# A two-layer streaming encoder: the stick-breaking products as three of 64 columns, summed in one bank, and the gate applied in VectorE's last step

## The chip, the cores and the metric

The kernel runs on one core of a Trainium2 chip. The metric is the device time of one execution in microseconds; before the change it is 1565.58 us, the median of 3 runs (1564.21 to 1566.16). What is read below comes from one profiled execution of the same kernel.

## The reference, cut to what matters

The trunk has two layers. The even layer (layer 0) has 4 heads of differential attention and 8 heads of stick-breaking attention, the odd one latent attention. The change touches the stick-breaking heads alone:

```python
z = einsum('bqhd,bkhd->bhqk', qb, ks) * (B_DH ** -0.5)          # B_DH = 64, 8 heads
earlier = pos[None, :] < tq[:, None]
log_skip = where(earlier, log_sigmoid(-z), 0.0)
log_pass = lax.cumsum(log_skip, axis=3, reverse=True) - log_skip
a = where(earlier, exp(log_sigmoid(z) + log_pass), 0.0)
ys = einsum('bhqk,bkhd->bqhd', a, vs).reshape(bsz, L, B_W) * silu(gs)
```

1024 tokens and 16 learned meta tokens make 1040 queries and keys. Everything is float32.

## The kernel before, in words

**Precision.** TensorE multiplies numbers of reduced precision at full rate. So every float32 operand is split into a high part (a rounded copy) and a low part (the rest), and a product is made as high x high, high x low and low x high, added up in a PSUM bank. ScalarE writes the high parts, VectorE the low ones (`ring`, `kst`, `qst`, `vtok`); GpSimd splits the weights of the projections (`wraw` to `wsp`, lines 872 and 873).

**Units and groups.** Layer 0 is worked in 8 units; units 0 to 3 (kind A) are the differential heads, units 4 to 7 (kind B) hold two stick-breaking heads each. A unit has one group for the 16 meta queries and four for pairs of query blocks (0 and 1, 2 and 3, 4 and 5, 6 and 7), and in kind B each of these once per head: 40 groups, numbers 20 to 59. Layer 1 (kind C) has 8 units.

**A kind B group.** TensorE makes the scores (line 1625). ScalarE takes the sigmoid (`tb`, line 1108). VectorE runs a product scan backwards over the keys (`pb`, line 1396); its result is the weight of "not yet taken", and with values replaced by differences of neighbours (GpSimd, `step_values`) the sum over keys gives the output but for the last value (`vlast`). The weights are turned by TensorE in turns of one or two key tiles (line 1649); ScalarE writes the turned high part into `ring` (line 1139), VectorE the low part (line 1411). Then TensorE multiplies (`product`, line 1679) into bank 7 (`PO`). In a kind B group the stationary operand is 128 columns wide: 64 of the values' high part, 64 of their low part. It is multiplied by the high part and by the low part of the weights, two instructions per key tile. Rows 0 to 63 of the bank then hold high values x all weights, rows 64 to 127 low values x all weights. The first turn of a group is the 16-row tile of the meta keys; the others have 128 rows. The last pair of a group has a tile of 256 query columns and one of 128, the other pairs have two of 256.

**The end of a group.** ScalarE copies rows 64 to 127 to `otmp` (`output`, line 1149, behind the semaphore `pv_done`), VectorE adds rows 0 to 63, `vlast` and `otmp` in one instruction per block and writes `ot` (line 1438, semaphore `o_evac`); the next group's first product waits for `o_evac`. After the second head of a pair, GpSimd multiplies 128 rows of `ot` by `gate` (`gate_group`, line 946, semaphore `y_gated`), and SyncE stores them. `gate` is the SiLU of the unit's own projection `g0`, made in three column chunks during the same unit: ScalarE takes the sigmoid (line 1065), VectorE multiplies (line 1283).

**Order.** Each engine runs its own list, in order. The lists come from a planner (`Lines`, `weave`): every step has an estimated duration, the steps that it waits for, and a tail, and the planner advances the engine that can begin first; `RANK` gives the precedence of kinds of step on an engine (S scores, T turning, X product, Y end of a group, G gating, W weight split, P projection's evacuation, p projection). Projection matmuls (line 1553) are put in one by one where TensorE has room. After the last projection of layer 0, GpSimd splits the eight tiles of the output weights (into `big`) and the first tiles of y, which are loaded back from `y_scratch`; then TensorE starts the output projection (line 1703).

## Time and profile before

| what | us |
|---|---|
| median of 3 runs | 1565.58 |
| profiled execution, its own time | 1564.86 |
| its span, first to last instruction | 1563.1 |
| TensorE matmuls busy in it | 1420.8 (91%) |
| VectorE, ScalarE, GpSimd busy | 850.1, 557.2, 525.2 |
| granted TensorE clock, share of full speed | 0.953 |

"Busy" is time in which at least one instruction of the engine runs; matmuls overlap, so the mean duration of one (some 300 ns) is not the distance to the next. That distance is read from a timeline: the start of one row of equal matmuls to the start of the next row, over their count. PE is TensorE, PEld its weight loads, DVE VectorE, ACT ScalarE, POOL GpSimd, SP SyncE. Layer 0's attention ends with the last projection near 711 us and the output projection's start near 750 us; layer 1 follows.

### The profile page before, as it was taken

The numbers are of one execution on the slowest core, as the hardware profiler recorded it, in microseconds if no ns is written. First come the engines' busy times: TensorE is split into PE (matmuls) and PEld (weight loads), VectorE is DVE, ScalarE is ACT, GpSimd is POOL, SyncE is SP. The second block draws the span as 40 slices with busy tenths as digits, with TensorE's granted clock in tenths as the row PEclk, the third lists the DMA queues.
The fourth block names the chain that finished last, engine by engine and source line by source line (L and its number), as shares of the span: only waits on it lengthen the run. The fifth ranks groups of instructions, "written<-read, shape, count | busy, mean of one in ns | idle before, by whom it ended". The sixth has DMA issues, their size and how long they took to land.

```text
span 1563.1 us, 22642 instructions
## 1 busy us (share of the span) xinstructions
PE 1420.8 (91%) x8604; PEld 1289.7 (83%) x8604; DVE 850.1 (54%) x1941; ACT 557.2 (36%) x1267; POOL 525.2 (34%) x426
## 2 busy tenths in 40 slices
PE   6999898989899999997899998998998989898896
PEld 6898797979788988986688997897887979887685
DVE  4666758585576746566244213424666656656243
ACT  3444344443544535253011004333344444434111
POOL 3213121212223042227544332532223222235553
PEclk9999998999999999997899999998999989989898
DMA  5000100000110010103433211111101111112541
GB/s 189 28 28 28 41 28 29 27 28 28 41 35 21 21 48 18 38 18 88 142 132 109 95 55 54 56 62 52 44 29 34 45 38 35 42 41 83 167 148 68
DMA packets 50796, 90.39 MB, mean 58 GB/s; under 512 B 4720, under 2 KB 33648, under 8 KB 50560
## 3 DMA queue, kind: packets, MB, share of 16 engines
q1 hardware_dynamic: 48384, 80.55, 16.0%
q10 hardware_dynamic: 2304, 8.39, 1.3%
q8 instruction: 69, 1.13, 0.3%
q14 instruction: 39, 0.32, 0.1%
HBM read 67.82 MB, written 21.10 MB: 57 GB/s over the span
## 4 chain that ended last, share of the span: by engine, by line
PE 44%; POOL 4%; DVE 4%; ACT 2%; issue 2%; DMA 1%; POOLq 0%; SPq 0%; ACTq 0%; DVEq 0%
PE bank L1553 17%; PE bank L1703 12%; PE bank L1625 7%; PE bank L1679 5%; PE bank L1649 2%; POOL big L873 2%; POOL big L872 1%; ACT rtmp L1079 1%; DVE qpe L1313 1%; PE bank L1576 1%; DVE qpe L1309 1%; DVE rtmp L1259 1%; DMA wraw<-y_scratch 1%; DVE rtmp L1257 0%; DVE rtmp L1258 0%
## 5 line engine op out<-in xcount | busy, mean ns | idle before, releaser
L1553 PE MATMUL bank<-big,wsp 128*128 128x344 f32 (+1 forms) x3024 | 583.5, 336 | 49.0 <-DVE qpe L1313 26.4
L1553 PEld LDWEIGHTS bank<-big,wsp 128*128 128x128 f32 x3024 | 495.3, 194 | 60.2 <-issue 22.1
L872 POOL TENSOR_SCALAR wsp<-wraw 128x1024 fp32r<-128x1024 f32 (+2 forms) x92 | 83.7, 910 | 495.4 <-PE bank L1553 416.9
L1679 PE MATMUL bank<-ring,vtok 128*128 128x256 f32 (+3 forms) x1276 | 206.1, 299 | 10.2 <-DVE ot L1438 4.8
L1411 DVE TENSOR_TENSOR ring<-bank,ring 16x256 fp32r<-16x256 f32 (+3 forms) x292 | 154.9, 550 | 109.7 <-ACT ring L1139 107.1
L1703 PE MATMUL bank<-big,wsp 128*128 128x512 f32 x816 | 195.7, 401 | 18.0 <-POOL wsp L873 18.0
L1679 PEld LDWEIGHTS bank<-ring,vtok 128*128 128x128 f32 (+1 forms) x1276 | 178.7, 200 | 35.4 <-issue 22.8
L1139 ACT ACTIVATE ring<-bank 16x256 fp32r<-16x256 f32 (+3 forms) x292 | 136.2, 487 | 191.5 <-PE bank L1649 116.4
L1703 PEld LDWEIGHTS bank<-big,wsp 128*128 128x128 f32 x816 | 155.7, 192 | 54.5 <-POOL wsp L873 18.3
L873 POOL TENSOR_TENSOR wsp<-wraw,wsp 128x1024 fp32r<-128x1024 f32 (+2 forms) x92 | 185.9, 2020 | 7.7
L1553 PE MATMUL bank<-h1t,wsp 128*128 128x344 f32 (+1 forms) x1080 | 174.7, 322 | 3.7 <-DVE kpe L1304 2.2
L1553 PEld LDWEIGHTS bank<-h1t,wsp 128*128 128x128 f32 x1080 | 171.2, 188 | 6.1 <-DVE kpe L1304 2.4
L1649 PE MATMUL bank<-eye,pb 128*128 128x128 f32 (+2 forms) x892 | 133.7, 281 | 8.7 <-DVE ring L1411 3.7
L1625 PE MATMUL bank<-kst,qst 128*128 128x264 f32 (+9 forms) x480 | 116.3, 340 | 22.2 <-POOL qst L913 11.2
L1649 PEld LDWEIGHTS bank<-eye,pb 128*128 128x128 f32 (+2 forms) x892 | 99.2, 135 | 18.1 <-DVE pb L1390 5.2
L1129 ACT ACTIVATE pb<-bank,stat 128x144 f32<-128x144 f32 (+6 forms) x112 | 59.8, 539 | 141.0 <-DVE stat L1370 81.8
L1625 PEld LDWEIGHTS bank<-kst,qst 128*128 128x128 f32 x480 | 81.7, 198 | 33.0 <-POOL qst L913 15.0
L975 POOL TENSOR_SCALAR pb<-pb,stat 128x144 f32<-128x144 f32 (+3 forms) x64 | 48.6, 760 | 158.2 <-DVE stat L1404 93.6
L1396 DVE TENSOR_TENSOR_SCAN pb<-tb 128x144 f32<-128x144 f32 (+4 forms) x72 | 91.6, 1295 | 14.8 <-ACT tb L1108 7.7
L1468 DVE SCALAR_TENSOR_TENSOR res<-xres,bank 128x512 f32<-128x512 f32 (+1 forms) x34 | 21.8, 684 | 116.8 <-PE bank L1703 111.3
L1351 DVE TENSOR_REDUCE stat<-bank 128x1 f32<-128x144 f32 (+6 forms) x112 | 56.8, 508 | 51.3 <-PE bank L1629 33.4
L1625 PE MATMUL bank<-kh,qh 128*128 128x144 f32 (+6 forms) x336 | 82.0, 355 | 2.4 <-ACT pb L1129 2.3
(115 smaller groups left out, 1493.9 us busy)
## 6 DMA issues: line engine op xcount, KB each, us to landing
wraw<-in_w SPq DMA_DIRECT2D x47, 512.0 KB, 3.5
wraw<-y_scratch SPq DMA_DIRECT2D x17, 512.0 KB, 5.3
wraw<-in_wo SPq DMA_DIRECT2D x16, 512.0 KB, 3.6
y_scratch<-ot SPq DMA_DIRECT2D x48, 128.0 KB, 1.8
gate_scratch<-gtmp SPq DMA_DIRECT2D x8, 520.0 KB, 2.9
gate<-gate_scratch SPq DMA_DIRECT2D x8, 520.0 KB, 3.6
xres<-in_x SPq DMA_DIRECT2D x8, 512.0 KB, 6.1
h_scratch<-res ACTq DMA_DIRECT2D x8, 512.0 KB, 4.7
```

The source lines that it names most:

```text
L872: pool.wait_ge(S["pool_step"], tick(nc.gpsimd.tensor_scalar(hi, raw, 1.0, 1.0, ALU.mult, ALU.mult)))
L873: return nc.gpsimd.tensor_tensor(lo, raw, lo_hi(hi), ALU.subtract)
L1129: A(pb1[:, g % 2, slot, c0:c0 + w], bank[S_BANK[b]][:, 0:w], ACT.Exp, bias=st_(6, 7), scale=SCALE192, accum_out=st_(8 + c, 9 + c)).then_in ...
L1139: A(R[0:rows, r % NRING, 0, 0:w], bank[T_BANK[t]][0:rows, 0:w], ACT.Copy).then_inc(S["tr_hi"], 1)
L1351: V.reduce_max(mx, src, AX_X).then_inc(S["dve_step"], 1)
L1396: V.tensor_tensor_scan(P[:, 0:n][:, ::-1], skip[:, ::-1], skip[:, ::-1], 1.0, ALU.mult, ALU.bypass)\
L1411: V.tensor_tensor(R[0:rows, r % NRING, 1, 0:w], bank[T_BANK[t]][0:rows, 0:w], lo_hi(R[0:rows, r % NRING, 0, 0:w]), ALU.subtract).then_inc( ...
L1553: ins = mm(dst, wsp[:, SLOT[kind, u], a, k, :], rhs[:, b, k0 + k, c0:c0 + w], start=(k == 0 and a == 0 and b == 0), stop=last)
L1625: ins = mm(dst, l, r, start=(k == 0), stop=(k == len(prods) - 1 and not masked))
L1649: ins = nc.tensor.transpose(bank[T_BANK[t]][0:wide, at:at + rows], weights[0:rows, g % 2, slot, k0:k0 + wide], eye[0:rows, 0:rows])
L1679: ins = mm(PO[:, o0:o0 + wide], l, B["ring"][0:rows, r % NRING, part, at:at + wide], start=(k == 0 and tile == turns[0][0] and part == 0 a ...
L1703: ins = mm(dst[:, :], wsp[:, SLOT["y", n], a, k, :], wok[:, c, k, 512 * half:512 * half + 512], start=(k == 0 and a == 0 and c == 0), stop ...
```

## The change

In kind B groups the stationary operand becomes 64 columns wide, and a tile takes three instructions (high values x high weights, low values x high weights, high values x low weights), all into rows 0 to 63 of the bank. ScalarE's copy to `otmp`, GpSimd's `gate_group` and the semaphores `o_tmp` and `y_gated` go. VectorE's step adds `vlast` and multiplies by `gate` at once; for that it waits for the gate's projection (`proj_evac`) and for `pv_done` itself. The planner is told the new durations and waits.

```diff
-RANK = {... "pool": "CDGQW", "sp": "FL"}
+RANK = {... "pool": "CDQW", "sp": "FL"}
@@ weave @@
-            L.put("pe", "X", x, (2 if kind == "B" else 3) * 0.46 * cols + 20 * n,
+            L.put("pe", "X", x, 3 * 0.46 * cols + 20 * n,
...
-            L.put("act", "Y", y, 300, [("pe", ring[-1]), over], 100)
-            L.put("dve", "Y", y, 600, [("act", y), ("sp", ("F", A_UNITS - 1)) if u == A_UNITS else None,
+            L.put("dve", "Y", y, 600, [("pe", ring[-1]), ("sp", ("F", A_UNITS - 1)) if u == A_UNITS else None,
+                                       evacuated(("P", "g0", u, min(chunk_of(i) for i in blocks))),
+                                       evacuated(("P", "g0", u, max(chunk_of(i) for i in blocks))),
                                        ("sp", stored[-2]) if head == 0 and len(stored) > 1 else None], 90)
             if head:
-                L.put("pool", "G", y, 700, [("dve", y), evacuated(...), evacuated(...)], 70)
-                L.put("sp", "F", y, 65, [("pool", y)], 2500)
+                L.put("sp", "F", y, 65, [("dve", y)], 2500)
@@ gpsimd: gate_group() goes, with its waits @@
-                nc.gpsimd.tensor_tensor(ot[:, c0:c0 + w], ot[:, c0:c0 + w], gate[:, c0:c0 + w], ALU.mult)\
-                    .then_inc(S["y_gated"], 1)
@@ scalar: output() goes @@
-                A(otmp[:, 0:w], PO[64:128, 0:w], ACT.Copy).then_inc(S["o_tmp"], 1)
@@ vector: output() @@
-                    dve.wait_ge(S["o_tmp"], B_GROUPS.index(g) + 1)
+                    for i in blocks:
+                        dve.wait_ge(S["proj_evac"], PTURN["P", "g0", u, chunk_of(i)] + 1)
+                    dve.wait_ge(S["pv_done"], RING[g, len(turns_of(blocks)) - 1] + 1)
...
                         ins = V.scalar_tensor_tensor(out=O[rows, c0 + at.start:c0 + at.stop], in0=PO[0:64, at],
-                                                     scalar=vlast[:, u % 2, head, last:last + 1], in1=otmp[:, at],
-                                                     op0=ALU.add, op1=ALU.add)
+                                                     scalar=vlast[:, u % 2, head, last:last + 1],
+                                                     in1=gate[rows, c0 + at.start:c0 + at.stop],
+                                                     op0=ALU.add, op1=ALU.mult)
@@ tensor: product() @@
                         if kind == "B":
-                            prods = [v[0:rows, u % 2, head, tile, :]]
+                            prods = [v[0:rows, u % 2, head, tile, DH * a:DH * a + DH] for a in ((0,) if part else (0, 1))]
...
-                            ins = mm(PO[:, o0:o0 + wide], l, ...
+                            ins = mm(PO[0:DH if kind == "B" else 128, o0:o0 + wide], l, ...
```

The lists of all engines are the same up to the first kind B product and from the output projection of layer 0 on. In between the planner makes another order. In the fences below, `bank<-ring,vtok` are products, `bank<-eye,pb` turned weights, `bank<-big,wsp` projections, `bank<-kst,qst` and `bank<-mask,eyebf` scores; lines of the changed kernel are some 30 lower (1648 for 1679, 1522 for 1553, 1618 for 1649, 1594 for 1625, 866 and 867 for 872 and 873, 905 for 913).

TensorE in unit 5, the two groups of blocks 2 and 3 (head 0, then head 1), before:

```order
L1679 MATMUL bank<-ring,vtok 128x256 x7
L1679 MATMUL bank<-ring,vtok 128x128
L1679 MATMUL bank<-ring,vtok 128x256
L1679 MATMUL bank<-ring,vtok 128x128
L1553 MATMUL bank<-big,wsp 128x352 x2
L1649 MATMUL bank<-eye,pb 16x128 x2
L1553 MATMUL bank<-big,wsp 128x352 x2
L1553 MATMUL bank<-big,wsp 128x344 x3
L1649 MATMUL bank<-eye,pb 128x128 x8
L1553 MATMUL bank<-big,wsp 128x344 x27
L1679 MATMUL bank<-ring,vtok 128x256 x7
L1679 MATMUL bank<-ring,vtok 128x128
L1679 MATMUL bank<-ring,vtok 128x256
L1679 MATMUL bank<-ring,vtok 128x128
```

and now:

```order
L1648 MATMUL bank<-ring,vtok 64x256 x11
L1648 MATMUL bank<-ring,vtok 64x128 x2
L1648 MATMUL bank<-ring,vtok 64x256
L1648 MATMUL bank<-ring,vtok 64x128
L1618 MATMUL bank<-eye,pb 16x128 x2
L1522 MATMUL bank<-big,wsp 128x344 x5
L1648 MATMUL bank<-ring,vtok 64x256 x3
L1522 MATMUL bank<-big,wsp 128x344 x2
L1648 MATMUL bank<-ring,vtok 64x256 x8
L1648 MATMUL bank<-ring,vtok 64x128 x2
L1648 MATMUL bank<-ring,vtok 64x256
L1648 MATMUL bank<-ring,vtok 64x128
```

The first group's products are followed by 34 projection matmuls before the second's begin, now by 5 and 2 more.

TensorE around the last projection of layer 0, before:

```order
L1553 MATMUL bank<-big,wsp 128x344 x2
L1649 MATMUL bank<-eye,pb 128x128 x3
L1553 MATMUL bank<-big,wsp 128x344 x4
L1649 MATMUL bank<-eye,pb 16x128 x2
L1553 MATMUL bank<-big,wsp 128x344 x3
L1649 MATMUL bank<-eye,pb 128x128 x4
L1553 MATMUL bank<-big,wsp 128x344 x7
L1679 MATMUL bank<-ring,vtok 128x256 x11
L1679 MATMUL bank<-ring,vtok 128x128
L1679 MATMUL bank<-ring,vtok 128x256
L1679 MATMUL bank<-ring,vtok 128x128
```

and now:

```order
L1598 MATMUL bank<-mask,eyebf 128x128
L1648 MATMUL bank<-ring,vtok 64x256 x11
L1648 MATMUL bank<-ring,vtok 64x128 x2
L1648 MATMUL bank<-ring,vtok 64x256
L1648 MATMUL bank<-ring,vtok 64x128
L1618 MATMUL bank<-eye,pb 16x128 x2
L1522 MATMUL bank<-big,wsp 128x344 x4
L1648 MATMUL bank<-ring,vtok 64x256 x11
L1648 MATMUL bank<-ring,vtok 64x128 x2
L1648 MATMUL bank<-ring,vtok 64x256
L1648 MATMUL bank<-ring,vtok 64x128
L1618 MATMUL bank<-eye,pb 128x128 x11
```

Before, the first products behind the last projection matmul are those of unit 7, head 0, blocks 4 and 5; now they are those of head 1, blocks 2 and 3, so one group more is left. In all, 64 products and 41 turned weights stand between the last projection and the output projection before, 111 and 58 now.

GpSimd at the same place, before:

```order
L913 TENSOR_SCALAR qst<-qst 64x2x344 x4
L946 TENSOR_TENSOR ot<-ot,gate 128x16
L946 TENSOR_TENSOR ot<-ot,gate 128x256
L872 TENSOR_SCALAR big<-wraw 128x1024
L873 TENSOR_TENSOR big<-wraw,big 128x1024
L872 TENSOR_SCALAR big<-wraw 128x1024
L873 TENSOR_TENSOR big<-wraw,big 128x1024
L946 TENSOR_TENSOR ot<-ot,gate 128x256
L872 TENSOR_SCALAR big<-wraw 128x1024
```

and now:

```order
L905 TENSOR_SCALAR qst<-qst 64x2x344 x4
L866 TENSOR_SCALAR big<-wraw 128x1024
L867 TENSOR_TENSOR big<-wraw,big 128x1024
L866 TENSOR_SCALAR big<-wraw 128x1024
L867 TENSOR_TENSOR big<-wraw,big 128x1024
```

The multiplies (`ot<-ot,gate`) are gone from between the splits (`big`).

## Rows read from the trace of the kernel before

**Rows 1.** The page, its first part: busy time, share of the span, instructions
```profile
PE 1420.8 (91%) x8604; PEld 1289.7 (83%) x8604; DVE 850.1 (54%) x1941; ACT 557.2 (36%) x1267; POOL 525.2 (34%) x426
```

**Rows 2.** The table of stretches: us, busy us (count) of PE PEld DVE ACT POOL, PEclk, DMA, GB/s
```profile
425.00:711.00 286.00, 274.88 (x1825) 251.52 (x1823) 178.36 (x298) 124.53 (x301) 79.99 (x70) 0.99 0.09 29
711.00:750.00 39.00, 21.08 (x106) 18.67 (x107) 19.21 (x29) 10.71 (x21) 37.81 (x21) 0.66 0.45 126
```

**Rows 3.** Waits of PE, then of POOL, 425 to 711 us: total us, times, longest
```profile
PE bank L1625 <- POOL qst L913: 5.3, 4, 2.6
PE bank L1553 <- POOL wsp L873: 3.2, 1, 3.2
PE bank L1679 <- DVE ot L1438: 1.4, 2, 1.2
...
POOL ot L946 <- DVE ot L1438: 84.6, 10, 22.9
POOL wsp L872 <- PE bank L1553: 57.7, 8, 11.7
```

**Rows 4.** The chain that ended last, 709 to 751 us: start us, us, what
```profile
710.81 2.83 POOL big L872
...
716.08 1.01 POOL big L872
...
719.54 0.68 POOL ot L946
...
725.44 3.03 POOL big L872
...
730.86 0.74 POOL ot L946
```

**Rows 5.** The timeline of PE, 709 to 751 us: start us, us, what, idle before
```profile
713.99 3.51 PE L1679 MATMUL bank<-ring,vtok 16*128 16x256 f32 x14 [3.34 <-DVE ot L1438]
...
749.73 1.65 PE L1703 MATMUL bank<-big,wsp 128*128 128x512 f32 x3 [11.52 <-POOL wsp L873]
```

**Rows 6.** The timeline of PE, around 483 and 605 us
```profile
483.14 1.11 PE L1679 MATMUL bank<-ring,vtok 128*128 128x256 f32 x8
484.10 0.49 PE L1649 MATMUL bank<-eye,pb 128*128 128x128 f32 x3
...
604.87 0.72 PE L1649 MATMUL bank<-eye,pb 128*128 128x128 f32 x5
605.34 0.41 PE L1553 MATMUL bank<-big,wsp 128*128 128x352 f32 x1
605.68 0.50 PE L1679 MATMUL bank<-ring,vtok 16*128 16x256 f32 x2
606.11 1.11 PE L1625 MATMUL bank<-kst,qst 128*128 128x456 f32 x4
...
607.10 0.65 PE L1679 MATMUL bank<-ring,vtok 128*128 128x256 f32 x4
607.59 1.82 PE L1553 MATMUL bank<-big,wsp 128*128 128x352 f32 x10
```

**Rows 7.** The weight loads by form: busy us, mean ns, idle before
```profile
L1649 PEld LDWEIGHTS bank<-eye,pb 128*128 128x128 f32 x720 | 85.4, 145 | 4.1 <-DVE ring L1411 0.7 <-issue 0.4
...
L1649 PEld LDWEIGHTS bank<-eye,pb 128*16 128x16 f32 x160 | 13.4, 90 | 12.2 <-DVE pb L1390 3.9 <-DVE pb L1396 3.5 <-POOL pb L975 1.8
```

**Rows 8.** Instructions by tile, otmp and ot: duration ns min/median/max
```profile
L1438 DVE SCALAR_TENSOR_TENSOR ot<-bank,vlast,otmp x72: 196/335/346, 432.5 to 739.0; 64x128 f32<-64x128 f32 x64, 64x16 f32<-64x16 f32 x8
L1149 ACT ACTIVATE otmp<-bank x40: 180/380/383, 398.3 to 738.2; 64x256 f32<-64x256 f32 x32, 64x16 f32<-64x16 f32 x8
...
L946 POOL TENSOR_TENSOR ot<-ot,gate x20: 221/730/742, 435.1 to 742.0; 128x256 f32<-128x256 f32 x16, 128x16 f32<-128x16 f32 x4
```

**Rows 9.** The timelines of DVE near 702 us and POOL near 525 us
```profile
701.91 1.78 DVE L1396 TENSOR_TENSOR_SCAN pb<-tb 128x784 f32<-128x784 f32 x1
...
525.63 0.92 POOL L946 TENSOR_TENSOR ot<-ot,gate 128x16 f32<-128x16 f32 x2 [15.35 <-DVE gate L1283]
```

More of the change, by code:

```diff
@@ L208 @@
 NEAR = {"pe": 0, "act": 0, "dve": 0, "pool": 0, "sp": 0}
-RANK = {"pe": "SXTVp", "act": "TSEYQP", "dve": "PTSMCYF", "pool": "CDGQW", "sp": "FL"}
+RANK = {"pe": "SXTVp", "act": "TSEYQP", "dve": "PTSMCYF", "pool": "CDQW", "sp": "FL"}
 class Lines:
@@ L357, in weave @@
         if kind == "B":
-            L.put("act", "Y", y, 300, [("pe", ring[-1]), over], 100)
-            L.put("dve", "Y", y, 600, [("act", y), ("sp", ("F", A_UNITS - 1)) if u == A_UNITS else None,
+            L.put("dve", "Y", y, 600, [("pe", ring[-1]), ("sp", ("F", A_UNITS - 1)) if u == A_UNITS else None,
+                                       evacuated(("P", "g0", u, min(chunk_of(i) for i in blocks))),
+                                       evacuated(("P", "g0", u, max(chunk_of(i) for i in blocks))),
                                        ("sp", stored[-2]) if head == 0 and len(stored) > 1 else None], 90)
             if head:
-                L.put("pool", "G", y, 700, [("dve", y), evacuated(("P", "g0", u, min(chunk_of(i) for i in blocks))),
-                                            evacuated(("P", "g0", u, max(chunk_of(i) for i in blocks)))], 70)
-                L.put("sp", "F", y, 65, [("pool", y)], 2500)
+                L.put("sp", "F", y, 65, [("dve", y)], 2500)
                 stored.append(y)
@@ L429, in weave @@
             if kind == "g0" and c == 0 and u >= 1:
-                wait = [("dve", ("F", u - 1)) if u - 1 < A_UNITS else ("pool", ("Y", unit_groups(0, u - 1)[-1]))]
+                wait = [("dve", ("F", u - 1)) if u - 1 < A_UNITS else ("dve", ("Y", unit_groups(0, u - 1)[-1]))]
             if kind == "qr" and turn[s]:
@@ L560 @@
 B_GROUPS = [g for g in range(len(GROUPS)) if GROUPS[g][1] == "B"]
-GATED = {g: n + 1 for n, g in enumerate(g for g in B_GROUPS if GROUPS[g][3] == 1)}
 P_COUNT = [P_OWNER[:t + 1].count(P_OWNER[t]) for t in range(len(TSTEPS))]
@@ L631, in trunk_kernel @@
         sq = sb("sq", [128, TOK], F32, st)
-        otmp = sb("otmp", [64, 256], F32, st)
         vlast = sb("vlast", [64, 2, 2, NB + 1], F32, st)
@@ L691, in trunk_kernel @@
             w_raw_0 w_raw_1 w_ready proj_done proj_hi proj_evac q_copied lat_sq lsq_used lat_split
-            s_done s_free_dve s_free_act max_ready exp_done inverted v_stepped y_gated p_ready_dve p_ready_pool
-            tr_done tr_hi tr_lo pv_done o_tmp o_evac sq_done unit_done y_stored_0 y_stored_1
+            s_done s_free_dve s_free_act max_ready exp_done inverted v_stepped p_ready_dve p_ready_pool
+            tr_done tr_hi tr_lo pv_done o_evac sq_done unit_done y_stored_0 y_stored_1
             g_stored_0 g_stored_1 g_loaded lam_exp rope_in lnp_in res_in_0 res_in_1
@@ L815, in _ @@
                         c0, w = group_cols(s[1])
-                        if kind == "B":
-                            sp.wait_ge(S["y_gated"], GATED[s[1]])
-                        else:
-                            sp.wait_ge(S["o_evac"], s[1] + 1)
+                        sp.wait_ge(S["o_evac"], s[1] + 1)
                         dst, src = yd[layer, u, :, c0:c0 + w], bufs(layer)["ot"][:, c0:c0 + w]
@@ L937, in step_values @@
                 pool.wait_ge(S["v_stepped"], u - A_UNITS + 1)
-            def gate_group(g):
-                _, _, u, _, blocks = GROUPS[g]
-                c0, w = group_cols(g)
-                for i in blocks:
-                    pool.wait_ge(S["proj_evac"], PTURN["P", "g0", u, chunk_of(i)] + 1)
-                pool.wait_ge(S["o_evac"], g + 1)
-                nc.gpsimd.tensor_tensor(ot[:, c0:c0 + w], ot[:, c0:c0 + w], gate[:, c0:c0 + w], ALU.mult)\
-                    .then_inc(S["y_gated"], 1)
-                gated[0] = GATED[g]
             split_ = [0]
-            gated = [0]
             weighted = [0]
@@ L1063, in evacuate @@
                         else:
-                            act.wait_ge(S["y_gated"], GATED[unit_groups(0, u - 1)[-1]])
+                            act.wait_ge(S["o_evac"], unit_groups(0, u - 1)[-1] + 1)
                     ins = A(gate[:, cc], src[:, 0:w], ACT.Sigmoid)
@@ L1139, in turned_weights @@
                 A(R[0:rows, r % NRING, 0, 0:w], bank[T_BANK[t]][0:rows, 0:w], ACT.Copy).then_inc(S["tr_hi"], 1)
-            def output(g):
-                _, kind, _, _, blocks = GROUPS[g]
-                if kind != "B":
-                    return
-                w = META if blocks == [META_Q] else 256
-                act.wait_ge(S["pv_done"], RING[g, len(turns_of(blocks)) - 1] + 1)
-                act.wait_ge(S["o_evac"], g)
-                A(otmp[:, 0:w], PO[64:128, 0:w], ACT.Copy).then_inc(S["o_tmp"], 1)
             def norm_block(s):
@@ L1198, in _ @@
                     turned_weights(*s[1:])
-                elif s[0] == "Y":
-                    output(s[1])
                 elif s[0] == "SQ":
@@ L1678, in product @@
                         for j, l in enumerate(prods):
-                            ins = mm(PO[:, o0:o0 + wide], l, B["ring"][0:rows, r % NRING, part, at:at + wide],
+                            ins = mm(PO[0:DH if kind == "B" else 128, o0:o0 + wide], l, B["ring"][0:rows, r % NRING, part, at:at + wide],
                                      start=(k == 0 and tile == turns[0][0] and part == 0 and j == 0),
```

4 lines of the change are left out of this document (removed).

## Prediction

> **What bounds the kernel now.** I read the page first: TensorE holds 91% of the span, VectorE 54%, the other two about a third [rows 1]. Then the table of stretches. The instruction streams of before and of the change part at the first product of the stick-breaking units (4 to 7) and meet again at the output projection of layer 0, so only the two middle stretches can change. From 425 to 711 us TensorE is busy for 274.9 of 286 us: it is the bound there, its three largest waits sum to 9.9 us, and of these only 1.4 us wait for the VectorE step that the change touches [rows 2, 3]. From 711 to 750 us something else rules: the chain of waits runs on GpSimd alone, from the end of the last projection (its first split starts at 710.81) through weight splits, two gate multiplies and a load [rows 4], until TensorE starts the output projection at 749.73. TensorE meanwhile has finished the last products by 738.2 and waits 11.52 us [rows 5].
>
> **The added products on TensorE.** A turn (one or two key tiles) before takes two instructions per tile: 128 stationary columns, high and low part of the values together, against the high and then the low part of the weights. Now it takes three of 64 columns. Over 8 head passes 400 products become 600. I count from the order how many stand ahead of the last projection: 208 of 256 columns with 128 rows, 56 of 256 columns with 16 rows, 56 of 128 columns and 16 of 16 columns become 303, 81, 81 and 24. The rest stands in the tail, 64 before and 111 now, and is taken below.
>
> The width of the stream sets the cadence, and it doesn't shrink with the stationary columns: eight 256-column products start within 0.96 us (483.14 to 484.10), 0.12 us each; four of a last pair, two of 256 and two of 128 columns, take 0.49 us (607.10 to 607.59) [rows 6]. The full pairs go from 152 to 222 products: 70 x 0.12 = +8.4 us. The last pairs go from 28 turns of 0.49 to 27 turns of six products. By stream alone (0.12 and half of it) a turn would be 0.54, by the old cadence x 1.5 it would be 0.74; so +0.9 to +6.3, and I take +2.4 (0.60 each), since a 64-column load should be the shorter one.
>
> The 16-row products are the odd ones: two start within 0.43 us, 0.215 each, although they stream 256 columns like the others [rows 6]; the load is not hidden there. In the rows of TensorE's weight loads a 128-column load of the transposes takes 145 ns and a 16-column one 90 ns [rows 7], so load time falls with columns, 0.49 ns each. A 64-column load then saves 0.03 to 0.05 us of the 0.215. 81 x 0.175 against 56 x 0.215: +2.1 us; bounds +1.3 (0.165) and +5.4 (nothing saved). The page "TensorE: Matmul & The Clock Gate" of the Trainium skill (section "LDWEIGHTS (loading the stationary operand)") says that a load's time is its columns over 1.2 GHz, whatever the rows. That makes 53 ns instead of 107. This trace's transposes fall by 0.49 ns a column, where the page has 0.83 [rows 7], so it agrees in kind and not in size. By the page the 16-row term would be +1.0.
>
> The eight extra 16-column products add some 0.12 each, +1.0 (bounds 0.9 and 1.7: the cadence of a transpose, 0.109, and the 0.215). 17 transposes leave this stretch for the tail, 0.109 each (five within 0.47 us, 604.87 to 605.34 [rows 6]): -1.9. Sum ahead of the last projection: 8.4 + 2.4 + 2.1 + 1.0 - 1.9 = +12.0 us. The granted clock is 0.99 in this stretch [rows 2], so no factor.
>
> **What is taken away.** 40 ScalarE copies (380 ns) and 20 GpSimd multiplies (730 ns) go; the 72 VectorE steps stay and keep their 335 ns: same sizes, one operand from the bank, one from SBUF [rows 8]. ScalarE and GpSimd are idle for half of the stretch and more, so the copies and multiplies are worth nothing by their busy time. As a hop they count: TensorE's next product waits for the copy and then for VectorE. That hop of some 0.5 us is covered by projections: 1.4 us of visible wait in 286 is all that can be won [rows 3], and I take 0, because of the next paragraph. GpSimd waits 84.6 us at its multiplies for VectorE's step [rows 3], and what is queued behind them are weight splits and query copies; TensorE waits 8.5 us for these. But most splits begin when a projection on TensorE frees their slot [rows 3], and that stays; I take 0 of the 8.5 and keep it for a rival.
>
> **What moves.** The VectorE step now waits for the gate's own projection, for head 0 as well. Before, that wait stood on GpSimd and nothing but GpSimd stood still (15.35 us at 525.63 [rows 9]). Behind it on VectorE now stand the low halves of the turned weights and the scans, and TensorE's next group of products waits for it. So the planner puts the products of a unit behind the gate's projections: in unit 5 the two groups of blocks 2 and 3 had 34 projection matmuls between them, now 7, and long runs of projections without products follow. Projections were the cover of every group's change-over. A change-over costs the two VectorE steps (0.6), what VectorE has begun before (a scan of 1.78 us [rows 9]) and the semaphores. Before, bare of cover, one showed as 3.34 us at 713.99 [rows 5]. I add +1 us for stalls (bounds 0 and 9: none, or half of 20 bunched change-overs at 0.9 us).
>
> **The tail (711 to 750).** The chain on GpSimd loses two multiplies, 0.68 and 0.74 us (the third of this stretch runs beside the load of y): -1.4, so 37.6 us from the last projection to the output projection if TensorE is ready [rows 4]. Nothing else in it changes: splits, one load of y, one more split. Two of the splits' first halves shown take 2.83 and 3.03 us, another 1.01; such a long one can fall elsewhere or go. TensorE was done after 27.4 us. It now has 47 more products and 17 more transposes there. At 2.4 GHz that is 47 x 0.12 + 17 x 0.11 = 7.5 us; at 1.2 GHz it is twice that, 15 (the granted clock is 0.66 over this stretch, a mixture of the two: 106 matmuls filled 21.1 us, 0.20 each [rows 2]). Less 4 x 0.5 us for the missing copy, TensorE is ready after 33 to 40.5 us, by the mixture's 0.20 after 38, beside GpSimd's 37.6. So the tail is 37.6 to 41 us instead of 39: -1 is my value, bounds -1.4 and +2.
>
> **Sum.** +12.0 + 1 - 1 = +12 us on the profiled execution's 1564.9 us (span 1563.1 and 1.8 around it): 1576.9. That execution lies 0.7 below the median of the runs; I forecast 1577. Its own range: with every low bound (+9.6, no stalls, -1.4) 1573, with the high ones of the products (+19.9), 1 us of stalls and +2 in the tail 1588.
>
> **Rivals.** (a) *Faster: GpSimd's queue is free.* With no multiply to stand at, splits and query copies start as soon as their inputs are there, and the 8.5 + 1.4 us of TensorE's waits vanish [rows 3]; with the low bounds of the products (8.4 + 0.9 + 1.3 + 0.9 - 1.9 = +9.6) and -1.4 in the tail: 1564.9 + 9.6 - 9.9 - 1.4 = 1563; with the long first halves of the splits gone as well, two of 2 us, 1559. I put it at 1561. For it: 84.6 us of waiting at the multiplies. Against: 57.7 us of GpSimd's other waits end at TensorE itself [rows 3], so most splits wait for slots, not behind the multiplies. 10%.
> (b) *Nearly the same.* The products cost their low bounds and half of those waits goes: 1564.9 + 9.6 - 5 - 1.4 = 1568. 14%.
> (c) *Slower than forecast: the bunches and the tail decide.* Stalls of 9 us in the bunches, and TensorE, not GpSimd, ends the tail at 1.2 GHz, +2: 1564.9 + 12 + 9 + 2 = 1588. It decides from the point where VectorE's step comes more than a turn's worth of transposes (0.5 us) after the last product. For it: 3.34 us at the only change-over without cover. Against: the order keeps transposes of the next group between. 18%.
> (d) *64-column products behave as the 16-row ones do.* Then no load hides, each 256-column product costs 0.215 - 0.04 = 0.175 or more, and each turn pays to enter and to leave: at 605.34 one projection matmul before two 16-row products lasts 0.34 us instead of 0.18 [rows 6]. 222 x 0.055 + 81 x 0.055 + 81 x 0.05 = +21 over my sum, and 64 turns x 0.3 = +19: 1617. Against: the last two of the five transposes at 604.87 have 16 stationary columns and start on the same beat as the 128-column ones [rows 6, 7]. 7%. The page "TensorEngine Tiling (Array Packing)" (section "Key Properties") says that a change of tiling mode drains TensorE, which speaks for (d) if a 64-column product counts as another mode; the 16-row products agree with it, the 16-column transposes don't.
>
> **How the numbers follow.** The forecast has 51%. Range 1564 to 1590: it holds the forecast, (b) and most of (c), some 79% in all, and leaves out (a), (d) and the far end of (c). A difference of 0.2% (3.1 us) is about what this measurement can tell from no change. Faster 10% (a, 1561 and less). Same 14% (b). Slower 76% (the forecast, c and d).
>
> **What would show it.** The profile after has 8804 matmuls, 200 more than the 8604 of before [rows 1]; the 256-column products start 0.12 us apart and the 16-row ones 0.17 to 0.2; the stretch from 425 us to the last projection is 299 us long instead of 286; GpSimd's chain from there to the output projection is near 38 us, and TensorE's wait before the output projection has shrunk from 11.52 us to under 2. No ScalarE copy of 380 ns stands there any more. I am wrong if 256-column products are 0.17 us apart or more (d), if TensorE's waits for VectorE's step sum to over 5 us (c), or if its waits for GpSimd fall from 8.5 to near 0 (a).

## The result and the profile after

The changed kernel takes 1585.64 us, the median of 4 runs (1580.93 to 1586.96); before stands at 1565.87 us beside it (4 runs, 1564.21 to 1567.43). The ratio is 1.0121 with a 95% interval of 1.0098 to 1.0144: slower by 20 us. The forecast was 1577, its range 1564 to 1590. Direction and range held; the size did not: 12 us were forecast and 20 measured. The profiled execution took 1585.76 us (span 1583.6), 20.9 more than before's, so it stands for the runs.

The page's busy line, to set beside [rows 1]:

```profile
PE 1437.4 (91%) x8804; PEld 1303.5 (82%) x8804; DVE 861.4 (54%) x1941; ACT 542.9 (34%) x1227; POOL 522.5 (33%) x406
```

The 200 more matmuls are there, and 40 ScalarE and 20 GpSimd instructions are gone. TensorE's busy time grew by 16.6 us, the span by 20.5. The table of stretches, cut at the last projection and at the output projection (columns as in [rows 2]):

```profile
425.00:728.00 303.00, 285.87 (x1962) 260.90 (x1961) 181.95 (x292) 110.32 (x263) 76.51 (x53) 0.97 0.09 28
728.00:768.00 40.00, 23.12 (x170) 19.64 (x169) 27.13 (x35) 10.55 (x20) 38.02 (x18) 0.79 0.42 124
```

The first stretch is 17 us longer than the 286 of before, where 13 were forecast (299). Of these 17, TensorE was busy for 11.0 (285.87 against 274.88) and idle for 6.0 (17.1 against 11.1). Now TensorE's waits in it (total, times, longest), against [rows 3]:

```profile
PE bank L1522 <- POOL wsp L867: 14.1, 3, 5.0
PE bank L1594 <- POOL qst L905: 2.9, 2, 1.5
```

This is the first surprise. The wait for VectorE's step, which the prediction watched, is gone; the wait of projections for GpSimd's split weights has grown from 3.2 to 14.1 us. Three timeline rows of TensorE are these waits (start, length, what, idle before):

```profile
465.04 1.25 PE L1522 MATMUL bank<-big,wsp 128*128 128x352 f32 x3 [4.96 <-POOL wsp L867]
...
560.71 2.71 PE L1522 MATMUL bank<-big,wsp 128*128 128x352 f32 x8 [4.57 <-POOL wsp L867]
...
657.14 3.30 PE L1522 MATMUL bank<-big,wsp 128*128 128x352 f32 x10 [4.56 <-POOL wsp L867]
```

They lie 96 us apart, one in each of units 4, 5 and 6. Look at the middle one. GpSimd's timeline there:

```profile
555.74 2.49 POOL L866 TENSOR_SCALAR wsp<-wraw 128x1024 fp32r<-128x1024 f32 x1 [39.73 <-PE bank L1522]
558.32 2.34 POOL L867 TENSOR_TENSOR wsp<-wraw,wsp 128x1024 fp32r<-128x1024 f32 x1
```

GpSimd had been waiting 39.73 us for TensorE: the slot that it wants to fill is freed only by the last matmul of the keys' projection. Then it needs 4.9 us, and the values' projection, which uses these weights, is what TensorE has next. TensorE just before it, in the changed kernel:

```profile
551.17 4.01 PE L1522 MATMUL bank<-big,wsp 128*128 128x344 f32 x24
...
555.15 0.40 PE L1522 MATMUL bank<-big,wsp 128*128 128x344 f32 x1
555.49 0.66 PE L1618 MATMUL bank<-eye,pb 128*128 128x128 f32 x4
```

and at the same place before:

```profile
546.83 1.06 PE L1679 MATMUL bank<-ring,vtok 128*128 128x256 f32 x8
547.73 1.48 PE L1649 MATMUL bank<-eye,pb 128*128 128x128 f32 x12
552.38 1.77 PE L1553 MATMUL bank<-big,wsp 128*128 128x352 f32 x7 [3.17 <-POOL wsp L873]
```

Before, 8 products and 12 turned weights stood between the keys' last projection matmul and the values' first; now 4 turned weights do. So the hole was there before, partly filled; the new order empties it. In the units before and after this one it was full before (23 and 32 matmuls), and now 3 and 4 stand there.

The second part of the price is the clock. Four stretches of the table, behind the first wait and then before, behind and past the second:

```profile
464.40:468.00 3.60, 2.96 (x13) 2.65 (x13) 3.60 (x2) 0.00 (x0) 3.52 (x3) 0.53 0.44 143
...
552.00:560.00 8.00, 4.14 (x28) 3.67 (x26) 7.85 (x9) 1.42 (x4) 4.17 (x2) 1.00 0.00 0
560.10:566.90 6.80, 6.19 (x21) 5.47 (x22) 3.34 (x3) 0.00 (x0) 5.94 (x3) 0.50 0.25 80
567.00:575.00 8.00, 8.00 (x68) 7.57 (x68) 4.65 (x10) 3.84 (x8) 0.00 (x0) 1.00 0.24 82
```

Around the end of a wait of 4.6 to 5 us the granted clock falls to half (1.2 instead of 2.4 GHz) for 3.4 or 6.8 us. Read from the clock's own records, 17.1 us of this stretch pass at half clock, against 6.8 us before. Each fall begins 0.6 to 1.5 us before TensorE resumes, so 2.7 of the 17.1 us are waiting, and TensorE works at half clock for 14.3 us. The table of stretches for the projections' line alone shows what that costs; of before, then of after:

```profile
425.00:711.00 286.00, 171.20 (x906) 143.95 (x904) 0.99 0.09 29
```

```profile
425.00:728.00 303.00, 178.85 (x906) 148.54 (x904) 0.97 0.09 28
```

The same 906 matmuls are busy for 7.7 us longer. (Busy times of lines overlap one another, so they don't add up to the engine's.) The products' line, of before, then of after:

```profile
425.00:711.00 286.00, 54.77 (x334) 45.05 (x334) 0.99 0.09 29
```

```profile
425.00:728.00 303.00, 62.71 (x488) 51.31 (x489) 0.97 0.09 28
```

154 more products take only 7.9 us more, 0.05 each. The tail, by the chain that ended last (start, length, what), against [rows 4]:

```profile
727.95 1.06 POOL big L866
...
732.56 4.13 POOL big L867
736.69 3.03 POOL big L866
...
760.29 3.76 DMA wraw<-y_scratch
```

GpSimd's chain from the last projection to the output projection is 39.7 us (727.95 to 767.65) against 38.9, and TensorE's wait before the output projection has gone from 11.52 to 5.7 us. The wait for VectorE's step, gone from the first stretch, stands here: 6.5 us in one piece, where it was 3.3 before [rows 5].

```profile
767.65 1.65 PE L1672 MATMUL bank<-big,wsp 128*128 128x512 f32 x3 [5.71 <-POOL wsp L867]
```

```profile
PE bank L1648 <- DVE ot L1406: 6.5, 1, 6.5
```

The last projection ends 17.1 us later, the output projection starts 17.9 us later, and layer 1 adds the last 2.6 us of the span. Its 4348 matmuls are the same; by the clock's records 70.2 us of it pass at half clock against 66.4, which is worth 1.9 of the 2.6.

### The profile page after: what moved, and what is told of

The parts are those of the page before. It is cut to its first block, busy times and chain, and to the rows that moved or that the text cites. A ratio compares the mean times of both kernels' runs of the same rounds, so it can differ in the third digit from the quotient of the medians.

```text
span 1583.6 us, 22937 instructions
## 1 busy us (share of the span) xinstructions
PE 1437.4 (91%) x8804; PEld 1303.5 (82%) x8804; DVE 861.4 (54%) x1941; ACT 542.9 (34%) x1227; POOL 522.5 (33%) x406
## 4 chain that ended last, share of the span: by engine, by line
PE 59%; POOL 6%; DVE 4%; ACT 2%; issue 2%; DMA 1%; POOLq 0%; SPq 0%; ACTq 0%; DVEq 0%
PE bank L1522 25%; PE bank L1672 12%; PE bank L1594 8%; PE bank L1648 8%; PE bank L1618 4%; POOL big L867 2%; POOL wsp L867 1%; ACT rtmp L1057 1%; POOL big L866 1%; DVE qpe L1279 1%; POOL wsp L866 1%; PE bank L1545 1%; POOL qst L905 1%; PE bank L1566 1%; PE bank L1598 1%
## 5 line engine op out<-in xcount | busy, mean ns | idle before, releaser
L1522 PE MATMUL bank<-big,wsp 128*128 128x344 f32 (+1 forms) x3024 | 591.3, 339 | 60.0 <-DVE qpe L1279 26.4
L866 POOL TENSOR_SCALAR wsp<-wraw 128x1024 fp32r<-128x1024 f32 (+2 forms) x92 | 92.6, 1007 | 634.3 <-PE bank L1522 555.9
L1648 PE MATMUL bank<-ring,vtok 128*128 128x256 f32 (+7 forms) x1476 | 214.6, 286 | 11.6 <-DVE ot L1406 6.5
L1648 PEld LDWEIGHTS bank<-ring,vtok 128*128 128x128 f32 (+3 forms) x1476 | 185.1, 172 | 38.0 <-issue 27.8
L1618 PE MATMUL bank<-eye,pb 128*128 128x128 f32 (+2 forms) x892 | 130.3, 278 | 9.6 <-DVE ring L1377 4.6
L1362 DVE TENSOR_TENSOR_SCAN pb<-tb 128x144 f32<-128x144 f32 (+4 forms) x72 | 102.5, 1448 | 11.6 <-ACT tb L1086 6.6
```

What stands on the lines that cost most here:

```text
L866: pool.wait_ge(S["pool_step"], tick(nc.gpsimd.tensor_scalar(hi, raw, 1.0, 1.0, ALU.mult, ALU.mult)))
L1362: V.tensor_tensor_scan(P[:, 0:n][:, ::-1], skip[:, ::-1], skip[:, ::-1], 1.0, ALU.mult, ALU.bypass)\
L1522: ins = mm(dst, wsp[:, SLOT[kind, u], a, k, :], rhs[:, b, k0 + k, c0:c0 + w], start=(k == 0 and a == 0 and b == 0), stop=last)
L1618: ins = nc.tensor.transpose(bank[T_BANK[t]][0:wide, at:at + rows], weights[0:rows, g % 2, slot, k0:k0 + wide], eye[0:rows, 0:rows])
L1648: ins = mm(PO[0:DH if kind == "B" else 128, o0:o0 + wide], l, B["ring"][0:rows, r % NRING, part, at:at + wide], start=(k == 0 and tile == ...
```

## The experiments

Each ratio is to before's runs on the same chip. Before's median was 1564.66 us beside the first four (11 runs), 1564.88 beside the next four (29 runs) and 1564.71 beside the last two (23 runs). "Price" is what the planner is told that a product costs.

**1. Three products, nothing else.** GpSimd keeps the gate, the planner keeps its numbers and so its order; ScalarE's copy goes, since nothing is left to copy.

```diff
-prods = [v[0:rows, u % 2, head, tile, :]]
+prods = [v[0:rows, u % 2, head, tile, DH * a:DH * a + DH] for a in ((0,) if part else (0, 1))]
...
-ins = V.scalar_tensor_tensor(out=O[...], in0=PO[0:64, at], scalar=vlast[...], in1=otmp[:, at], ...)
+ins = V.tensor_scalar(O[...], PO[0:64, at], vlast[...], None, ALU.add)
```

> The kernel before with the three 64-column products and without ScalarE's copy; VectorE adds the last value alone, GpSimd multiplies by the gate as before, and the planner keeps its old table, so the order is that of before. Theory T (of the change's +20 us the products cost some 8 to 9, the rest comes from the order: the product groups stand behind the gate's projections, and nothing is left beside the split of the value projection's weights): 1575 us, waits of TensorE for that split near 4 us in 425 to 720 us. Rival R (the products themselves, and that they are priced at three in the planner, make the whole): 1583 us or more.

Measured: 1573.16 us, ratio 1.0067 [1.0049, 1.0084]. Its waits of TensorE up to 705 us are those of before:

```profile
PE bank L1622 <- POOL qst L913: 5.3, 4, 2.6
PE bank L1550 <- POOL wsp L873: 2.4, 1, 2.4
```

The products by themselves, with ScalarE's copy gone, cost 8.5 us of the 20. The other 11 belong to the gate and the order. T forecast 1575 and a wait of 4 us; the total and the wait (2.4) both came out a little lower.

**2. The same, with the change's price.**

```diff
-            L.put("pe", "X", x, (2 if kind == "B" else 3) * 0.46 * cols + 20 * n,
+            L.put("pe", "X", x, 3 * 0.46 * cols + 20 * n,
```

> As e1_products_only, but the planner prices a kind B product at three as in the change (other order, gate still on GpSimd). T: 15 products still stand in front of the value projection, the waits for its weights stay under 7 us, 1576 us. R: the price makes the bunches, waits of 14 us and 1584 us.

Measured: 1578.58 us, ratio 1.0094 [1.0081, 1.0107]. No wait for split weights appears; TensorE's waits for VectorE are 4.2 (step) and 2.2 us (turned weights) up to 703 us instead. T's 1576 is nearer than R's 1584. The intervals of experiments 1 and 2 just overlap: that the higher price made this order worse is likely, not shown. The two traces differ in the clock: 13.7 us of this first stretch pass at half clock, 3.4 in experiment 1.

**3. The change with the old price.**

```diff
-            L.put("pe", "X", x, 3 * 0.46 * cols + 20 * n,
+            L.put("pe", "X", x, (2 if kind == "B" else 3) * 0.46 * cols + 20 * n,
```

> The changed kernel with the planner's old price of two for a kind B product; gate in VectorE's step. T: the wait for the gate's projection makes the order, so TensorE's waits for weight splits stay at 10 us or more and the time at 1582 to 1586 us. R: the price is what moved the order, so 1576 us.

Measured: 1586.21 us, ratio 1.0137 [1.012, 1.0153], as the change itself. The wait stays:

```profile
PE bank L1522 <- POOL wsp L867: 11.6, 3, 4.6
```

So the price did not empty the hole. What remains of the change is where the gate is applied.

**4. The gate on VectorE, with before's products.** ScalarE's copy and the two wide products stay; GpSimd's multiply goes, VectorE multiplies in an instruction of its own, behind the same waits as in the change, and the planner is told so. The main lines:

```diff
+                    for i in blocks:
+                        dve.wait_ge(S["proj_evac"], PTURN["P", "g0", u, chunk_of(i)] + 1)
                     dve.wait_ge(S["o_tmp"], B_GROUPS.index(g) + 1)
...
-                    ins.then_inc(S["o_evac"], 1)
+                    then(ins)
+                    V.tensor_tensor(O[rows, c0:c0 + w], O[rows, c0:c0 + w], gate[rows, c0:c0 + w], ALU.mult)\
+                        .then_inc(S["o_evac"], 1)
```

> The kernel before with its two 128-column products and ScalarE's copy, but VectorE multiplies by the gate (one more instruction per group and head) and waits for the gate's projection, planned so; GpSimd multiplies nothing. T: not one matmul stands beside the split of the value projection's weights in units 5 to 7, so TensorE waits some 15 us for splits in the stretch from 425 us: 1579 us. R: no added products, so 1566 to 1568 us.

Measured: 1578.48 us, ratio 1.0095 [1.0082, 1.0108]. The total is near T's; the way to it is not. The waits for split weights come back without any third product, but 7.8 us in 2, not some 15. In the table of stretches the first is only 0.8 us longer than before's, and the loss is in the tail:

```profile
425.00:711.79 286.79, 271.38 (x1771) 247.59 (x1770) 185.78 (x318) 118.74 (x287) 70.94 (x53) 0.97 0.09 29
711.79:762.62 50.83, 31.12 (x158) 24.99 (x158) 38.69 (x45) 15.76 (x33) 43.20 (x20) 0.73 0.32 91
```

The tail takes 50.8 us instead of 39. The output projection starts without a wait: TensorE, which stands 11.7 us at VectorE's step in the tail, ends it and not GpSimd. So half of T is confirmed (the gate's wait brings the hole) and its size is not.

**5 to 7. The gate's projection first.** A unit has two slots for split weights, used in turn. In units 4 to 7 the order was keys' first chunk, gate, keys' rest, values, queries; keys and values share a slot with nothing but the keys' own end between them. With the gate first, the slots are gate a, keys b, values a, queries b: the values' weights can be split while the keys' projection runs.

```diff
-            out += ... else k[:1] + norm + proj("g0", u) + k[1:] + v + q
+            out += ... else norm + proj("g0", u) + k + v + q
```

5, this line in the changed kernel:

> The changed kernel with another order of the projections in units 4 to 7: the gate's projection first and whole, then keys, values, queries (before: first chunk of the keys, gate, rest of the keys, values, queries). Two projections in a row then never share a weight slot, so the value projection's split runs beside the 72 matmuls of the keys. T (the extra loss over the products is the exposed split and the clock that falls after it): TensorE's waits for weight splits (14.1 us) go to under 2, no fall of the clock at 465, 560 and 656 us, 1569 to 1573 us. Rival R2 (the bunched groups themselves cost, whatever the split does): 1582 us or more.

6, in the kernel before:

> The kernel before with the same new order of projections. T: it had 3.2 us of that wait and one fall of the clock behind it, so 1560 to 1562 us. R2: no difference to before, 1565.

7, in the kernel of experiment 1:

> e1_products_only with the new order of projections. T: the products' own cost over e6_before_g0_first, +8 us: 1569 us. If the gate in VectorE's step is worth something of its own, e5_change_g0_first comes out below this one; T says the same within 3 us.

Measured: 5 takes 1561.32 us, ratio 0.9977 [0.9965, 0.9988]; 6 takes 1561.70, ratio 0.9977 [0.9965, 0.9988]; 7 takes 1571.23, ratio 1.0034 [1.002, 1.0048]. The stretches of 5, then TensorE's only wait in the first up to 703 us:

```profile
425.00:706.67 281.67, 278.64 (x1967) 256.62 (x1966) 175.68 (x291) 109.81 (x264) 67.46 (x52) 1.00 0.09 28
706.67:747.16 40.49, 23.26 (x170) 19.80 (x168) 27.19 (x35) 10.60 (x20) 38.06 (x19) 0.80 0.43 125
```

```profile
PE bank L1594 <- POOL qst L905: 2.9, 2, 1.5
```

This settles the hole. The changed kernel with one line moved is 24 us faster. Its first stretch is 21.3 us shorter, 14.1 of it idle time (3.0 against 17.1) and 7.2 busy time with 5 more records, at a clock of 1.00 instead of 0.97. None of it passes at half clock, where the change worked for 14.3 us at half, and half of that is 7.2: the wait and the clock behind it make the whole 21.3. GpSimd at the same place:

```profile
554.13 1.05 POOL L866 TENSOR_SCALAR wsp<-wraw 128x1024 fp32r<-128x1024 f32 x1 [19.10 <-PE bank L1522]
555.27 2.38 POOL L867 TENSOR_TENSOR wsp<-wraw,wsp 128x1024 fp32r<-128x1024 f32 x1
```

It splits while TensorE has projections and products in hand. For 5 I expected 1569 to 1573 and got more than that: under the new order the change is not slower than the kernel before, although its products still cost. 6 fell within its 1560 to 1562. Here are the first stretches of 6 and 7:

```profile
425.00:706.00 281.00, 273.19 (x1821) 251.08 (x1820) 178.09 (x295) 123.34 (x301) 80.87 (x69) 0.99 0.09 28
```

```profile
425.00:717.24 292.24, 286.29 (x2001) 262.29 (x1999) 177.75 (x297) 112.56 (x267) 82.81 (x70) 0.99 0.09 27
```

From 6 to 7 only the products (with ScalarE's copy) differ: 11.2 us here, 9.5 in the total. From 7 to 5 the gate's place and the price differ: 10.6 us back. Of these, 2.9 are idle time (5.95 to 3.03); some 3.7 are 15 products and 17 turned weights that went behind the last projection, into the shadow of GpSimd's chain (15 x 0.12 + 17 x 0.11, an estimate from the spacings in [rows 6]). Of the remaining 4 us, 3.4 are the clock: TensorE works for 6.8 us at half clock in 7, behind a wait of 2.56 us for GpSimd's query copies, and not at all in 5. Which of the two edits did it, experiment 10 tells. My expectation for 7, that it would equal 5 within 3 us, was wrong. And 5 ends level with 6 although its products take 8.6 us more (start to start, 55.8 against 47.1), because TensorE is idle for 3.0 us instead of 7.8, and at half clock for none of this stretch instead of 6.8 us.

**8. Queries before values, in the changed kernel.**

```diff
-            out += ... else k[:1] + norm + proj("g0", u) + k[1:] + v + q
+            out += ... else k[:1] + norm + proj("g0", u) + k[1:] + q + v
```

> The changed kernel with the query projection ahead of the value projection in units 4 to 7, all else as it was. The value projection's slot is then split beside the query projection. T: no wait for splits in front of the value projection, 9 to 14 us less wait ahead of the last projection. But 126 products and 67 turned weights are left behind the last projection (111 and 58 in the change), so the tail ends later, with TensorE, not with GpSimd: 1575 to 1582 us. R2: no gain ahead of the last projection.

Measured: 1581.99 us, ratio 1.0106 [1.0088, 1.0123], with the same wait as the change:

```profile
PE bank L1522 <- POOL wsp L867: 14.1, 3, 5.0
```

The time lies at the edge of T's 1575 to 1582, but by luck: the wait that T said would go is all there. The expectation was wrong because the experiment was: the slots go by turn, so whatever projection comes third, with the keys' as the first and the gate's as the second, takes the keys' slot. It does show that the hole belongs to the slot and its place in the order, not to the values.

**9. Experiment 4 with the gate's projection first.**

```diff
-            out += ... else k[:1] + norm + proj("g0", u) + k[1:] + v + q
+            out += ... else norm + proj("g0", u) + k + v + q
```

> Two products of 128 columns as before, with ScalarE's copy; VectorE adds, then multiplies by the gate in an instruction of its own; in units 4 to 7 the gate's projection stands ahead of the keys'. T (the gate on VectorE hurts only through the order of the projections, and products cost time): TensorE's waits for split weights of 7.8 us vanish, the last projection ends near 705 us, but the tail holds more products and is ended by TensorE as it was in the version without the new order, so about 1563, within 1558 to 1568. R (a VectorE step more is what costs): waits for VectorE's step of 5 us or more ahead of the last projection, and 1570 or above.

Measured: 1564.69 us, ratio 0.999 [0.9978, 1.0003]. TensorE has no wait for split weights up to 703 us, and 3.8 us (4 times) for VectorE's step, near R's 5. The total is within T's 1558 to 1568. By the table of stretches the last projection ends 7 us ahead of T's 705, and the tail is as T has it, ended by TensorE:

```profile
425.00:697.83 272.83, 265.60 (x1781) 243.04 (x1780) 186.12 (x317) 118.67 (x288) 67.84 (x53) 1.00 0.09 28
697.83:752.23 54.40, 32.99 (x159) 26.92 (x158) 41.92 (x45) 15.85 (x33) 42.88 (x20) 0.65 0.30 85
```

It is 13.8 us down on experiment 4 by the same one line, and its tail of 54.4 us, with TensorE at a clock of 0.65 and no wait before the output projection, is 13.9 us longer than that of experiment 5 (40.49), while its first stretch is 8.8 us shorter.

**10. Experiment 5 with the old price.**

```diff
-            L.put("pe", "X", x, 3 * 0.46 * cols + 20 * n,
+            L.put("pe", "X", x, (2 if kind == "B" else 3) * 0.46 * cols + 20 * n,
```

> The change with the gate's projection first in units 4 to 7, and the planner told the price of two products. T: no TensorE wait for split weights ahead of the last projection, as in the version priced at three; total within 3 us of its 1561.3. R (the price in the planner decides, as its effect on the unmoved order was +6 us either way): 1567 or more.

Measured: 1568.98 us, ratio 1.0022 [1.0008, 1.0035]. No wait for split weights, as T said; but 7.7 us above experiment 5, so T's "within 3" failed and R's 1567 or more held. The stretches:

```profile
425.00:712.77 287.77, 283.65 (x2000) 260.04 (x1998) 178.45 (x294) 111.19 (x266) 65.78 (x52) 1.00 0.09 27
712.77:754.66 41.89, 19.84 (x145) 17.27 (x143) 26.92 (x32) 9.52 (x18) 37.98 (x19) 0.77 0.43 131
```

33 more records stand ahead of the last projection and 25 fewer behind it, where TensorE now waits 9.10 us for GpSimd instead of 6.05. The first stretch is 6.1 us longer, 5.0 of it busy and 1.1 idle, and the tail 1.4 us longer; no part of either first stretch passes at half clock. With the price of experiment 7, this kernel differs from that one in the gate's place alone, and there the two are 2.2 us apart with intervals that overlap (1.0008 to 1.0035, and 1.002 to 1.0048). So most of the 10 us between 7 and 5 came from the price, through the order that it makes. That fits one reading, which no run tests by itself: work ahead of the last projection costs its time, and the same work behind it is free as long as GpSimd's chain of some 39 us is the longer one.

A third slot for split weights would be the other test of the cause. It was not tried, and whether the kernel's memory has room for one is not shown here. The one moved line also makes the planner weave everything else anew, so the 24 us are those of the new order as a whole; that the wait and its clock are the part that counts rests on the 21.3 us above.

## Why the prediction was right in sign and short in size

**Products (forecast +13.9 with everything added, before the moved transposes).** Too much. The line's busy time rose by 7.9 us, and alone (experiment 1) they cost 8.5 in the total. Start to start over all forms, idle time left out, they hold TensorE for 56.2 us against 47.1: +9.1. The cadence forecast held: start to start, a 256-column product takes 0.113 to 0.118 us after. What failed is that I priced the old ones at that cadence too. Summed over their records, the 208 of before hold TensorE for 29.8 us, 0.143 each: 31 of them took 0.19 us or more, 29 of these at most 0.22. Of the 31, 28 are the first 128-row product behind something else, where the next one then starts late: 23 behind a 16-row product, 3 behind a turned weight, 2 behind a mask. The 303 of after hold it for 35.8 us, 0.118 each, and none takes 0.19: the 18 latest, all the first behind a 16-row product, take 0.16 to 0.185. The weight loads point to the reason (busy us, mean ns, idle before), of before and of after:

```profile
L1679 PEld LDWEIGHTS bank<-ring,vtok 128*128 128x128 f32 x264 | 34.7, 190 | 3.8 <-DVE ring L1411 0.7
L1679 PEld LDWEIGHTS bank<-ring,vtok 16*128 16x128 f32 x70 | 10.4, 185 | 7.5 <-issue 6.3 <-ACT ring L1139 0.7
```

```profile
L1648 PEld LDWEIGHTS bank<-ring,vtok 128*64 128x64 f32 x384 | 41.0, 134 | 3.9 <-issue 3.5
L1648 PEld LDWEIGHTS bank<-ring,vtok 16*64 16x64 f32 x105 | 10.4, 132 | 7.0 <-issue 4.8 <-ACT ring L1117 1.9
```

A load of 128 columns takes 190 ns and one of 64 columns 134. That is 0.88 ns a column, not the 0.49 that I took from the transposes [rows 7]. What counts is when the loads start. At the start of a turn the second load starts 0.109 us behind the first with 128 columns (435.837 and 435.945) and 0.055 behind it with 64 (546.387 and 546.442), and its product follows it by 0.115 to 0.121 in both; further on, each load starts together with the product ahead of its own. So the first 128-row product behind a 16-row one is followed after some 0.22 us before and at most 0.185 now. The page "TensorE: Matmul & The Clock Gate" of the Trainium skill (section "LDWEIGHTS (loading the stationary operand)"), which makes it 0.83 ns a column, was the better guide here: the trace agrees with its slope, and the durations lie some 80 ns above its 107 and 53. So the narrower products won back part of what their number costs, on the 256-column ones and not only on the 16-row ones where I looked. Of those, three stand in a row now. The first is followed after 0.17 us, the second after 0.12 and the third, by something else, after 0.20 or 0.21; over all 83 the mean is 0.166, where 0.175 was forecast:

```profile
546.39 0.56 PE L1648 MATMUL bank<-ring,vtok 16*64 16x256 f32 x3
546.88 0.90 PE L1522 MATMUL bank<-big,wsp 128*128 128x344 f32 x4
```

The three take 0.49 us up to the projection behind them, 0.163 each, against 0.215 [rows 6]. Of the forecast for (d), products that cannot hide their load, nothing came.

**Moved transposes (-1.9).** 17 fewer stand ahead of the last projection, and start to start the turned weights take 28.55 us instead of 30.63: -2.1. The term held.

**Stalls (+1, bounds 0 and 9).** This is the step that failed: "most splits begin when a projection on TensorE frees their slot [rows 3], and that stays; I take 0 of the 8.5", and +1 for change-overs. The sentence on the slots was true and the conclusion was not. I had seen that the planner would gather projections into long runs, and asked only what that does to products (rival c). I didn't ask what it does to a wait that TensorE's other work had been covering: GpSimd's split between keys and values. That wait rose from 3.2 to 14.1 us while the others fell from 7.9 (11.1 less 3.2) to 3.0. Net idle time is +6.0, inside the bounds, for a cause that stood in none of the rivals: change-overs at VectorE's step, (c)'s mechanism, came to nothing in this stretch. In the tail one of them lasted 6.5 us, more than the 5 us that I had named as a sign of (c); but there TensorE still waits 5.7 us for GpSimd afterwards, so it did not set the end. Rival (a) had its waits for GpSimd reversed: they went from 8.5 to 17.0 us (14.1 and 2.9).

**The clock (no factor).** Second failed step. "The granted clock is 0.99 in this stretch [rows 2], so no factor" took the clock as given, though the traces have it fall around the longer waits: TensorE worked for 14.3 us at half clock instead of 6.8. At half speed a stretch does half its work, so the 7.5 us more cost about 3.8.

The four together, +9.1 for products, -2.1 for transposes, +6.0 idle and +3.8 for the clock, make +16.8, where the stretch grew by 17.0 and 13 were forecast. That the result lies in the range is partly luck: products came out 4.8 us under their term, idle time and clock 8.8 over theirs.

**The tail (-1, bounds -1.4 and +2).** +0.8. The two multiplies did go, but the splits stretched. Four halves in the chain are long (4.13, 3.03, 2.76 and 4.28 us, where 2.35 and 1.03 stand elsewhere in it), 7.4 us more than the short ones in all; before it was three (2.83, 2.76 and 3.03), 5.5 us more. TensorE's wait before the output projection shrank to 5.7, not under 2, so GpSimd still ends the tail, as forecast.

**What of the result is the change's own?** Its products, 8.5 to 9.5 us (experiments 1, and 7 against 6). The gate in VectorE's step, at one price in the planner, costs 13 us with the old order of projections (experiment 3 against 1, 1586.21 against 1573.16) and nothing that can be told with the new one (10 against 7, 1568.98 against 1571.23). The price of three is worth nothing with the old order (1585.64 against 1586.21) and 7.7 us with the new one (5 against 10). The best versions are 5 and 6, at 1561.3 and 1561.7 us, 0.2% faster than before (0.9977 [0.9965, 0.9988] both); they can't be told apart, so the change itself brings nothing that moving the projection doesn't.

## What to carry to other kernels

When a new wait makes a planner gather one kind of work, list the waits which that work, or the work it displaces, had been covering, on every engine: the hole opened at a buffer that the edit never touched. With two slots in turn, put something between the user of a slot and its next user that is longer than the refill (here 4.9 us, and 3.5 where no scan stands beside it, as in experiment 5). And price a duplicated instruction by the mean distance of its like over the whole stretch, not by the cadence of one clean row.

## What the runs showed of the hardware

- A single idle time of 4.6 to 5.0 us of TensorE in an otherwise busy stretch came with 3.4 or 6.8 us at half the granted clock each time, and the fall began before the idle time ended; one of 3.17 us before was followed by 3.4 us (553.1 to 556.6, clock 0.51), one of 2.57 us too (601.0 to 604.4). Over all the traces here, from 425 to 700 us, each of the 12 idle times of 3.1 to 5.0 us came with such a fall, and 7 of the 11 of 1.5 to 2.6 us; the stretches without any (experiments 5, 9 and 10) had no fall.
- GpSimd's split halves take 1.03 or 3.03 and 2.38 or 4.13 us for the same 128x1024 tile. The long ones lie beside VectorE's scans, which are long there as well (timeline of VectorE, changed kernel):

```profile
732.50 2.05 DVE L1362 TENSOR_TENSOR_SCAN pb<-tb 128x912 f32<-128x912 f32 x1
...
734.78 4.09 DVE L1362 TENSOR_TENSOR_SCAN pb<-tb 128x1040 f32<-128x1040 f32 x1
...
739.97 7.09 DVE L1362 TENSOR_TENSOR_SCAN pb<-tb 128x912 f32<-128x912 f32 x2
```

  A scan of 912 columns took 2.05 us, and 3.5 each for the two at 739.97, while GpSimd's 736.69 (3.03) to 749.25 ran. The times fit waiting for each other in turn, and not a lower speed of both: GpSimd's half of 732.56 ends at 736.69, 2.14 us after the end of the scan of 732.50; the scan of 734.78 ends at 738.87, 2.18 after the end of that half; the half of 736.69 ends at 739.72, 0.85 after the end of that scan. Each is near what it takes elsewhere in all (2.35, 2.30 and 1.03), as if it had only waited first. That is read from one trace's times; no run took one of the two away.
- 64 columns instead of 128 cut a weight load of these products from 190 to 134 ns, and where the first 128-row product behind a 16-row one was followed after 0.22 us (23 times), it is now after 0.16 to 0.185 (18 times) or in the normal beat.
